# The last block of an output projection taken tile by tile, with the turns and first logits of the router inside it

## What is computed

```python
    merged = jax.nn.sigmoid(gate_r) * y_ret + jax.nn.sigmoid(gate_m) * y_m
    return merged @ w_out
...
        x = x + hybrid_mixer(h, ...)
        h = rms_norm(x, norm_ffn_w[layer])
        x = x + hierarchical_moe(h, ...)
    return rms_norm(x, norm_final_w)
...
    group_prob = jax.nn.softmax(xf @ w_group + b_group, axis=-1)
    g_w, g_idx = lax.top_k(group_prob, 1)
    e_logits = (xf @ w_expert_router + b_expert_router).reshape(T, N_GROUPS, EXPERTS_PER_GROUP)
    sel_logits = e_logits[jnp.arange(T), g_idx[:, 0]]
    top_logits, e_idx = lax.top_k(sel_logits, TOP_K)
```

## Time and profile before

| | us |
|---|---|
| median of 3 runs | 1023.49 (1023.42 to 1024.78) |
| the profiled execution, its own time | 1022.9 |
| its span, first to last instruction | 1021.0 |
| TensorE busy | 996.3 (98%) |
| VectorE / ScalarE busy | 500.1 / 323.9 |
| block 21 on TensorE | 512.8 to 534.5 |
| turns, logits and logit rows on TensorE | 534.5 to 543.3 |
| first gather issued | 554.1 |
| first expert matmul | 561.3 |
| last expert matmuls of the last pair end | about 1004 |

### The profile page before, as it was taken

One profiled execution on the slowest core, in us unless ns is written; L12 is line 12 of the kernel. 1 busy time (PEld: TensorE's weight loads), 2 busy tenths in 40 slices (PEclk: granted clock), 3 DMA queues, 4 the chain that ended last, 5 costly groups with the idle time before them and its releaser, 6 DMA issues.

```text
span 1021.0 us, 13126 instructions
## 1 busy us (share of the span) xinstructions
PE 996.3 (98%) x4917; PEld 644.4 (63%) x4917; DVE 500.1 (49%) x810; ACT 323.9 (32%) x531; POOL 120.8 (12%) x152
## 2 busy tenths in 40 slices
PE   8999999999999999999998999999999999999896
PEld 7888788889889988888885333333333333333332
DVE  6268646597778677735525123333223233332235
ACT  6344535586556557622213100000000000000012
POOL 0683077000000000000000000000000000000000
PEclk9999999999999999999999999999999999999999
DMA  9223231344334525162988899999999999999993
GB/s 331 83 83 126 92 114 21 83 125 145 66 91 113 185 42 205 43 213 90 422 307 357 348 420 420 420 420 420 420 420 420 421 420 420 420 421 421 421 414 146
DMA packets 63125, 269.28 MB, mean 264 GB/s; under 512 B 9488, under 2 KB 9680, under 8 KB 38360
## 3 DMA queue, kind: packets, MB, share of 16 engines
q1 hardware_dynamic: 57464, 257.32, 63.6%
q0 software_dynamic: 5344, 11.02, 4.9%
q10 hardware_dynamic: 256, 0.10, 0.0%
HBM read 268.41 MB, written 4.20 MB: 267 GB/s over the span
## 4 chain that ended last, share of the span: by engine, by line
PE 72%; SPq 17%; DVE 5%; DMA 3%; ACT 2%; issue 1%; DVEq 0%; ACTq 0%
PE pj L674 23%; PE pj L854 18%; PE pj L956 12%; SPq L575 11%; PE pj L982 6%; SPq L572 6%; PE cb L631 3%; DMA raw_moe<-in_w_up_dram 3%; PE cb L992 2%; PE cb L993 1%; DVE mkT L1758 1%; DVE wl L1494 1%; PE cb L723 1%; PE cb L695 1%; ACT wh L1136 1%
## 5 line engine op out<-in xcount | busy, mean ns | idle before, releaser
L956 PE MATMUL pj<-raw_moe,xT 128*64 128x512 f32 x1016 | 227.6, 595 | 4.2 <-DMA raw_moe<-in_w_up_dram 2.4
L1494 DVE TENSOR_TENSOR wl<-raw_mix,wh 128x1024 fp32r<-128x1024 f32 x116 | 146.2, 1262 | 130.9 <-ACT wh L1136 130.6
L1970 DVE TENSOR_TENSOR x<-x,cb 128x512 f32<-128x512 f32 x120 | 77.0, 683 | 190.2 <-PE cb L993 190.2
L956 PEld LDWEIGHTS pj<-raw_moe,xT 128*64 128x64 f32 x1016 | 72.1, 137 | 140.8 <-issue 140.8
L1136 ACT ACTIVATE wh<-raw_mix 128x1024 fp32r<-128x1024 f32 x116 | 122.4, 1057 | 111.4 <-PE pj L674 68.5
L982 PE MATMUL pj<-raw_moe,hf 128*64 128x512 f32 x512 | 116.7, 598 | 1.6 <-ACT hf L1440 1.6
L982 PEld LDWEIGHTS pj<-raw_moe,hf 128*64 128x64 f32 x512 | 34.6, 136 | 67.2 <-issue 67.0
L1445 ACT ACTIVATE yh<-pj,now 128x512 fp32r<-128x512 f32 x32 | 20.4, 683 | 157.6 <-PE cb L993 143.6
L1440 ACT ACTIVATE hf<-cb 128x512 f32<-128x512 f32 x16 | 9.6, 598 | 146.3 <-PE cb L631 146.3
L992 PE MATMUL cb<-yh,hot 128*128 128x512 f32 x124 | 55.2, 445 | 0.0
L674 PE MATMUL pj<-wh,hTh 128*128 128x512 f32 x128 | 50.8, 397 | 1.7 <-DVE hTl L1525 0.7
(11 more groups left out here) (397 smaller groups left out, 1858.5 us busy)
## 6 DMA issues: line engine op xcount, KB each, us to landing
raw_moe<-in_w_gate_dram SPq DMA_DIRECT2D x64, 1024.0 KB, 26.7
raw_moe<-in_w_down_dram SPq DMA_DIRECT2D x64, 1024.0 KB, 26.7
raw_moe<-in_w_up_dram SPq DMA_DIRECT2D x63, 1024.0 KB, 26.0
raw_mix<-in_w_in_dram SPq DMA_DIRECT2D x31, 1024.0 KB, 5.3
raw_mix<-in_w_in_dram POOLq DMA_DIRECT2D x10, 512.0 KB, 5.8
raw_mix<-in_w_ret_branch_dram SPq DMA_DIRECT2D x4, 1024.0 KB, 5.8
raw_mix<-in_w_mlstm_branch_dram SPq DMA_DIRECT2D x4, 1024.0 KB, 5.5
raw_mix<-in_w_out_dram SPq DMA_DIRECT2D x4, 1024.0 KB, 5.1
```

The source lines that it names most:

```text
L956: mm = nc.tensor.matmul(pj[a * CAP:(a + 1) * CAP, up, :], xT[:, 4 * half + k, a * CAP:(a + 1) * CAP], weights_of(m + a)[:, k, :], start=ha ...
L1494: V.tensor_tensor(wl[:, q % RING, :, :], entry_source(q), wh[:, q % RING, :, :].bitcast(F32), ALU.subtract).then_inc(wl_ok, 1)
L1970: V.tensor_tensor(part, part, cb[:, 2 + g % 2, :], ALU.add).then_inc(c_add, 1)
```

## The change

The first 21 blocks run as before. Block 21 goes tile by tile: `stream_tile(i)` takes tile i through all four quarters, with the same 24 matmuls. The turns of a tile stand one tile behind its matmuls: tile 0, tile 1, turn 0, tile 2, turn 1, tile 3, turn 2, logit rows 0, turn 3, logits 1, logit rows 1. The first logits stand inside tile 3, after its second quarter. `turn_stream(2)` waits for the sums of tiles 0 and 1 too, whose banks it writes.

VectorE: the router's weights are prepared after the last residual instead of before it, and the copies of turned tiles stand between the sums. ScalarE: the copy of turn 1 goes ahead of the third square and the first logit columns are copied behind that square. SyncE: three stores of the stream go ahead of chunks 11, 12, 15 and 17, since the second quarter is now free only in tile 3.

```diff
@@ sync
-            sp.wait_ge(*entry_used(ENTRIES - 3))
-            for m in (11, 12, 15, 17):
-                moe_chunk(m, 0, False)
             for t in range(TT):
+                if t == TT - 1:
+                    sp.wait_ge(*entry_used(ENTRIES - 3))
+                    for m in (11, 12, 15, 17):
+                        moe_chunk(m, 0, False)
                 sp.wait_ge(free[t], free_of(t, BLOCKS - 1))
                 sp.dma_start(x_dram[t * P:(t + 1) * P, :], x2[:, t, :]).then_inc(st_in, 16)
@@ tensor
-            for b in range(B_WR, BLOCKS):
+            for b in range(B_WR, BLOCKS - 1):
                 block_of(b)
             def turn_stream(t):
-                pe.wait_ge(free[t], free_of(t, BLOCKS - 1))
+                for i in (0, 1, t) if t == 2 else (t,):
+                    pe.wait_ge(free[i], free_of(i, BLOCKS - 1))
...
+            def stream_tile(i):
+
+                b = BLOCKS - 1
+                pe.wait_ge(free[i], free_of(i, b - 1))
+                cols = slice(i * P, (i + 1) * P)
+                for j in range(4):
+                    q = entry(b, j)
+                    if i == 0:
+                        pe.wait_ge(wl_ok, q + 1)
+                    for kk in range(2):
+                        k = 2 * j + kk
+                        ops = ((mrgTh[:, k, cols], wh[:, q % RING, kk, :]), (mrgTl[:, k, cols], wh[:, q % RING, kk, :]),
+                               (mrgTh[:, k, cols], wl[:, q % RING, kk, :]))
+                        for n, (lhsT, rhs) in enumerate(ops):
+                            m = nc.tensor.matmul(pj[:, i, :], lhsT, rhs, start=k == 0 and n == 0, stop=k == KD - 1 and n == 2)
+                    if j == 3:
+                        m.then_inc(full[i], 1)
+                    elif i == 3:
+                        m.then_inc(pair_used, 1)
+                    if i == 3 and j == 1:
+                        pe.wait_ge(wrt_ok, 1)
+                        logits(0)
+
+            stream_tile(0)
+            stream_tile(1)
             pe.wait_ge(tr_l, 2 * KD)
-            for t in range(TT):
-                turn_stream(t)
-            pe.wait_ge(wrt_ok, 1)
-            logits(0)
+            turn_stream(0)
+            stream_tile(2)
+            turn_stream(1)
+            stream_tile(3)
+            turn_stream(2)
+            logit_rows(0)
+            turn_stream(3)
             logits(1)
-            logit_rows(0)
             logit_rows(1)
@@ scalar
+            def logits_copy(u):
+                act.wait_ge(lgT_ps, 2 * u + 2)
+                nc.scalar.activation(lgT[:, 256 * u:256 * (u + 1)], cb[:, u, 256 * u:256 * (u + 1)], ACT.Copy).then_inc(lgT_ok, 1)
...
             stream_copy(0)
+            stream_copy(1)
             square(2)
-            stream_copy(1)
+            logits_copy(0)
             stream_copy(2)
             square(3)
             stream_copy(3)
             root(5, TT)
-            for u in range(2):
-                act.wait_ge(lgT_ps, 2 * u + 2)
-                nc.scalar.activation(lgT[:, 256 * u:256 * (u + 1)], cb[:, u, 256 * u:256 * (u + 1)], ACT.Copy).then_inc(lgT_ok, 1)
+            logits_copy(1)
@@ vector
-            evict_block(BLOCKS - 1)
...
+            stream_sum(0)
+            stream_sum(1)
+            stream_turned(0)
+            stream_sum(2)
+            stream_turned(1)
+            stream_sum(3)
+            stream_turned(2)
+            stream_turned(3)
```

More of the change, by code:

```diff
@@ L1683, in evict_block @@
                         V.tensor_tensor(sgm[:, ct, :], pj[:, i, :], sgm[:, ct, :], ALU.mult).then_inc(free[i], 1)
-                    if p in (B_WO, B_WO + 1):
+                    if p == B_WO:
                         half = slice(512 * (p - B_WO), 512 * (p - B_WO + 1))
@@ L1716, in block_of @@
                     V.tensor_copy(iot[:, :], kc[:, K_SLOT:K_SLOT + CAP]).then_inc(it_ok, 1)
[L1717 to L1722, removed]
                 if b == B_MQ:
@@ L1889, in _, with stream_sum, stream_turned @@
                 block_of(b)
-            evict_block(BLOCKS - 1)
-            for t in range(TT):
+            def stream_sum(t):
+                dve.wait_ge(full[t], full_of(t, BLOCKS - 1))
+                V.tensor_tensor(x2[:, t, 512:D], pj[:, t, :], x2[:, t, 512:D], ALU.add).then_inc(free[t], 1)
+            def stream_turned(t):
                 dve.wait_ge(h2T_ps, 2 * t + 1)
@@ L1896, in _ @@
                 V.tensor_copy(h2T[:, 0:4, t * P:(t + 1) * P], bank.rearrange("p (k n) -> p k n", k=4)).then_inc(h2T_v, 1)
+            dve.wait_ge(br_in, 128)
+            V.tensor_tensor(wrt[:, :, 0:36], wrt[:, :, 0:36], nwc[:, :].unsqueeze(2).to_broadcast([P, KD, 36]), ALU.mult)
+            V.memset(wrt[:, :, 36:HALF], 0.0)
+            V.tensor_tensor(fold[:, :], kc[:, K_IDENT:K_IDENT + HALF], kc[:, K_IDENT + HALF:K_IDENT + P], ALU.add).then_inc(wrt_ok, 1)
+            stream_sum(0)
[6 more added lines that the diff above has]
+            stream_turned(3)
             dve.wait_ge(sq_ok, 4 * TT)
```

## The result

| | median us | runs | profiled execution: span |
|---|---|---|---|
| before | 1023.37 | 6 (1021.94 to 1024.78) | 1021.0 |
| changed | 1029.45 | 6 (1028.99 to 1030.19) | 1028.2 |

The ratio is 1.0061, 95% interval 1.0048 to 1.0073; between the medians the changed kernel is 6.1 us slower. The forecast of 1026.4 us had the direction, but the measured time lies above its range of 1024.2 to 1028.6.

The account below looks back on a forecast made before the run. TensorE and the expert weight stream, both starting from the first gate matmul, were taken as the bound. Late routing 1.3 us plus gather 1.6 gave +2.9: 1023.49 + 2.9 = 1026.4 us, range 1024.2 to 1028.6.

Parts of the forecast that it names:

- The start alone prices the change: First gate matmul at 561.27 us starts TensorE's pairs and weight refills; moving it by d moves the end by d.
- two of the signs that the prediction itself named for being wrong: Gather under 5.7 us, no holes at logits, clock below 1.00 in first gate, or expert stage changing length.
- TensorE's own work at 0: Block 21 to logit rows: same matmuls, transposes and logits, no hole to fill, so reordering gains 0.
- Waits at the logits: End of block 21: TensorE waits 0.86 us at second logits, 0.53 at second rows; routing +1.3 us, bounds 0.5 to 1.8.
- SyncE and the weights: Four chunks issued 10.1 us later, backlog done about 560.0, chunk 22 by 562.6; the bytes themselves cost 0.
- The first gather: After routing: issued at 555.45, takes 7.2 us instead of 4.7 beside late weights, bounds 4.7 to 8.5.
- the 1.6 us of this term: The first gather's share of the forecast 2.9 us delay of the first gate.
- I had estimated 6 us: First gather waiting for one packet of weights takes about 6 us, landing at 561.45; d would be 1.75 us.
- The clock: Rival, chance 0.15: TensorE's clock falls while waiting before the first gate, costing 1.7 us; d 4.6, 1028.1 us.
- The wait that I forecast myself, 1.6 us: TensorE idle 1.6 us before turning the first gathered rows, ahead of the first gate.

Follow-up runs that it names:

- the two kernels in which the weights ended with nothing queued behind them: Guest chunk and chunk 22 held until the first gather landed: changed kernel so edited 1024.93 us; with first logits also back behind the turns 1024.78 us.
- the first group: One chip's runs: SyncE's part alone, guest chunk and chunk 22 held, seven keep-busy matmuls, logits behind the turns; kernel before beside them 1022.65 us.

## Why the prediction was wrong in size

**The start alone prices the change: right only while the clock stays up.** In the kernels whose first gate runs at clock 1.00 the end moved one for one with the first gate, within 0.6 us, and in the changed kernel the weight stream kept its hole (0 GB/s at 566 to 569 us). But there the gate ran at 0.50 and the part behind it grew by 1.4 us, two of the signs that the prediction itself named for being wrong.

**TensorE's own work at 0: nearly.** Block 21 with what stands in it takes 538.78 + 0.23 - 513.12 = 25.89 us where the sum gave 25.49. Of the 0.4 us, each change from turns or logits back to the block's matmuls leaves about 0.1 us.

**Waits at the logits: right.** 0.86 and 0.53 us were forecast, 0.91 and 0.48 came. With the 0.4 us above the routing starts 1.85 us late, not 1.3, just above the upper bound of 1.8. What these waits are worth in the changed kernel stays open: without them the median of four runs was no lower.

**SyncE and the weights: right.** The four chunks were forecast from 533.8 and came at 534.38; full flow was to end at 562.6 and ended at 564.3. Chunk 22 went 0.7 us later with the routing, and the stream ran at only 254 and 279 GB/s in the two stretches from 544 to 546 us.

**The first gather: the step that failed.** I took 7.2 us, shortening 8.5 because after 562.6 nothing competes, and called 8.5 the upper bound. It took 9.2 us and 8.4 us in the two profiles of the changed kernel. The case with only chunk 22 held shows the reasoning wrong: the weights ended 2.7 us before the landing and it still took 8.0 us, because 2.5 us of the excess lie ahead of the first row, and the end of the weights came after it. The row with the weights flowing should have been taken whole, and with its spread: later gathers of the kernel before took up to 9.7 us. Instead of the 1.6 us of this term there were 3.5. The row of 3.4 us was no guide either: the second gather moves 0.18 MB, the first 0.29. By the Trainium skill's rule (DMA: Bandwidth & Descriptors, Queues, rings and completion order: a DMA engine takes turns between queues a packet at a time) I had estimated 6 us; 8.0 to 9.2 us in the five kernels whose weights flowed to 561 us or later do not bear that number out. Nor do the rows support the working of the 6 us: the trace shows a chunk as 128 packets of 8 KB, which is eight an engine if they are spread evenly, where I had counted 16 descriptors, and 2.5 us of the excess lie ahead of the first row.

**The clock: named, but as a rival.** I gave 0.15 to a fall of the clock behind TensorE's idle time and priced it at 1.7 us. It fell in the profiled execution of every kernel in which TensorE waited over 2.4 us for the gather, and the part behind the first gate was 1.2 to 2.2 us longer there than in the kernel before. The wait that I forecast myself, 1.6 us, was too short to make me take it in; with the gather's true length it was no longer a side case. I counted two dependent terms apart: the longer gather brought the clock with it.

The sum, corrected by the profiled executions: 1.85 + 3.47 + 0.12 + 1.42 = 6.86 us; with the 0.34 us ahead of the change it is the 7.2 us between the two spans, beside 6.1 us between the medians.

## What to carry to other kernels

A transfer issued off the critical path can still be felt there, when it makes the queues busy at the moment a small latency-bound transfer is due: ask of each delayed prefetch what it will run beside, not only whether it arrives in time. Price such a small transfer by the row in which it really ran in traffic, and add what the engine's clock costs if the wait becomes long. Where an engine's chain has no hole before the change, there is nothing for moved work to fill; here moving it opened two, of 0.91 and 0.48 us.

## What the runs showed of the hardware

The first gather (0.29 MB, 70 rows of 4 KB) took 4.4 to 4.8 us with the weights just ended or just starting, 5.3 and 6.5 us in the two kernels in which the weights ended with nothing queued behind them, 2.6 and 2.2 us before it landed, and 8.0 to 9.2 us otherwise, 8.0 in the kernel in which the weights ended 2.7 us before it landed but behind the guest chunk. The second (0.18 MB) took 3.4 to 3.7 us in the stream's hole and 6.5 us in the two kernels in which the held weights had started again. All later ones, in the stream, took 7.8 to 9.7 us.

The issue on GpSimd took 1.4 us for every first gather, so it is not what grew. The first row of the first gather moved 2.1 us after the issue where no weights flowed, 2.2 and 3.9 us after it in the two kernels in which the weights were running out, and 4.5 to 4.8 us after it where they flowed on; for the later gathers in the stream it was 4.1 to 4.4 us. What happens in that time is open; no run here shows it.

TensorE idle for 2.4 to 4.3 us ahead of the gathered rows was accompanied or followed by a granted clock of 0.50 in all five profiled executions that show it; idle for 0.9 us and less there it was not, in the other eight. How long the low level lasted differed between executions of one kernel, which is part of their spread. The kernel before has such a spread without the long wait: its runs beside the first group took 1022 to 1023.3 us at a mean clock of 0.996 to 0.998 and 1024.0 to 1024.8 at 0.993 and 0.994. The two runs of the kernel with the logits behind the turns at a mean clock of 0.990 were 1.0 to 2.1 us slower than the two at 0.995 and 0.996.
